# A streaming-encoder layer on one core: first two projection blocks split at token 256, loads re-ordered, square-root table loaded first

## What is computed

```python
def _rmsnorm(x, g):
    xf = x * rsqrt(mean(x * x, axis=-1) + EPS)
    return xf * g

h = _rmsnorm(x, norm_mix_pre)
c = h @ w_in        # 15 column blocks for RWKV-7, 12 for differential attention, 16 for the gates
```

## Time and profile before

| | us |
|---|---|
| median of 3 runs | 1066.26 (1065.84 to 1068.44) |
| the profiled execution, whole | 1068.19 |
| its span, first to last instruction | 1066.4 |
| PE busy / PEld busy | 1011.7 / 952.3 |
| DVE / ACT / POOL busy | 490.4 / 277.4 / 487.5 |
| granted TensorE clock, mean | 0.979 |

### The profile page before, as it was taken

The page is one execution under the profiler, slowest core; times in us unless marked ns, Lnnn a source line. Parts: engine busy times, 40 slices in busy tenths (PEclk is TensorE's granted clock), DMA queues, the critical chain, the costliest instruction groups (busy, mean ns, idle before and its releaser), DMA issues.

```text
span 1066.4 us, 21824 instructions
## 1 busy us (share of the span) xinstructions
PE 1011.7 (95%) x8886; PEld 952.3 (89%) x8886; DVE 490.4 (46%) x876; ACT 277.4 (26%) x782; POOL 487.5 (46%) x327
## 2 busy tenths in 40 slices
PE   4999999999879998989999999999999999999996
PEld 4999999977768887878799998999999999999996
DVE  5566799377767455555345254233323333200003
ACT  4223444345434123332211254010101010011101
POOL 3555566332215123142146811665655556566571
PEclk9999999999979999999889999999999999999998
DMA  7322323422213110103303621323323232322332
GB/s 240 84 81 79 84 76 81 132 81 71 64 33 85 43 32 13 52 32 115 109 26 119 190 73 41 96 81 88 89 80 97 79 98 79 91 79 86 92 90 85
DMA packets 137581, 89.16 MB, mean 84 GB/s; under 512 B 5242, under 2 KB 129504, under 8 KB 137504
## 3 DMA queue, kind: packets, MB, share of 16 engines
q1 hardware_dynamic: 128980, 72.65, 23.9%
q10 hardware_dynamic: 8524, 15.42, 4.2%
HBM read 78.86 MB, written 9.19 MB: 83 GB/s over the span
## 4 chain that ended last, share of the span: by engine, by line
PE 81%; DVE 12%; ACT 3%; issue 2%; POOL 1%; DMA 1%; ACTq 0%; DVEq 0%; POOLq 0%
PE dense L956 65%; PE side L1026 3%; PE side L882 1%; PE side L1146 1%; PE side L872 1%; DVE early L1645 1%; PE side L908 1%; PE side L1069 1%; PE side L938 1%; DVE amax L1629 1%; PE side L862 1%; DVE gt L1750 1%; DVE AR L1817 1%; ACT early L1260 1%; PE side L903 1%
## 5 line engine op out<-in xcount | busy, mean ns | idle before, releaser
L698 POOL TENSOR_SCALAR w_hi<-w_raw 128x1024 fp32r<-128x1024 f32 x117 | 128.0, 1094 | 440.5 <-PE dense L956 425.8
L956 PE MATMUL dense<-h_hi,w_hi 128*128 128x272 f32 (+1 forms) x1392 | 305.6, 297 | 7.9 <-DVE h_lo L1565 6.2
L956 PE MATMUL dense<-h_lo,w_hi 128*128 128x272 f32 (+1 forms) x1392 | 296.1, 290 | 0.0
L956 PE MATMUL dense<-h_hi,w_lo 128*128 128x272 f32 (+1 forms) x1392 | 294.7, 289 | 0.0
L701 POOL TENSOR_TENSOR w_lo<-w_raw,w_hi 128x1024 fp32r<-128x1024 f32 x117 | 285.7, 2442 | 9.8
L956 PEld LDWEIGHTS dense<-h_hi,w_hi 128*128 128x128 f32 x1392 | 222.2, 191 | 18.7 <-DVE h_lo L1565 6.9
L956 PEld LDWEIGHTS dense<-h_lo,w_hi 128*128 128x128 f32 x1392 | 224.1, 191 | 0.0
L956 PEld LDWEIGHTS dense<-h_hi,w_lo 128*128 128x128 f32 x1392 | 223.2, 191 | 0.0
L956 PE MATMUL dense<-S,w_hi 128*128 128x272 f32 (+2 forms) x648 | 109.3, 289 | 0.0
L956 PEld LDWEIGHTS dense<-S,w_hi 128*128 128x128 f32 x648 | 92.1, 188 | 0.1
L956 PE MATMUL dense<-S,w_lo 128*128 128x272 f32 (+2 forms) x324 | 68.2, 288 | 0.0
(11 more groups left out here) (265 smaller groups left out, 1423.6 us busy)
## 6 DMA issues: line engine op xcount, KB each, us to landing
w_raw<-in_w_ffn_in SPq DMA_DIRECT2D x44, 512.0 KB, 3.8
w_raw<-in_w_in SPq DMA_DIRECT2D x43, 512.0 KB, 3.9
w_raw<-in_w_ffn_out SPq DMA_DIRECT2D x16, 448.0 KB, 3.6
gates<-gst ACTq DMA_DIRECT2D x16, 272.0 KB, 2.0
w_raw<-in_w_o SPq DMA_DIRECT2D x8, 512.0 KB, 3.9
w_raw<-in_w_ffn_out SPq DMA_DIRECT2D x8, 512.0 KB, 3.8
mb<-gates ACTq DMA_DIRECT2D x1, 2176.0 KB, 10.7
ga<-gates ACTq DMA_DIRECT2D x1, 2176.0 KB, 10.8
```

The lines of the kernel that those rows point to most:

```text
L698: nc.gpsimd.tensor_scalar(hi, w_raw[:, slot, :], 1.0, 0.0, ALU.mult, ALU.add).then_inc(hi_split, 1)
L956: ins = pe.matmul(acc[:, bk, 0:tn], w, r[:, t0:t0 + tn], start=first and n == 0, stop=final and n == 2)
```

## The change

The two first blocks are cut at token 256 instead of 272. Their first part needs tiles 0 and 1 only, and it is 256 columns wide; the second is 288. In the list the first part of c0 moves to just behind B1, then come A3 and B2, the first part of c1, A4, B3, B4, and the two second parts. The list of ACT, DVE and POOL keeps its order; only PE's changes. SP issues x0, `gain`, x1, unit 0, x2, unit 1, x3, x4, and then the parameters. The squares throw their result into `tmp` in SBUF, so the wait for all square roots is gone. DVE sets `rms` to one at the start, ACT waits for it and takes a square root of it, ahead of the first square. ACT's three copies of the two blocks follow the new cut.

```diff
--- before.py
+++ after.py
@@ -198,16 +198,13 @@
 
         return [(st, i - k) for i in range(n + len(stages) - 1) for k, st in enumerate(stages) if 0 <= i - k < n]
 
-    def first_pair(steps, blocks):
-
-        halves = [("dense", *d, hf, BY_TOKENS) for hf in range(2) for d in blocks]
-        return steps[:-2] + halves[:1] + steps[-2:-1] + halves[1:2] + steps[-1:] + halves[2:]
-
     def spread(n, places):
 
         return [(i + 1) * n // places - i * n // places for i in range(places)]
 
-    s = first_pair(skew(NT, "normA", "normB"), [("c", i) for i in C_ORDER[:2]]) + [("params",)]
+    first_pair = [("dense", "c", i, hf, BY_TOKENS) for hf in range(2) for i in C_ORDER[:2]]
+    norms = skew(NT, "normA", "normB")
+    s = norms[:5] + first_pair[:1] + norms[5:7] + first_pair[1:2] + norms[7:] + first_pair[2:] + [("params",)]
     beside = {
         2: [("shift", CWA), ("loraW",)],
         3: [("shift", CK)],
@@ -526,7 +523,7 @@
     stored = sem("stored")
     kout_stored = [sem(f"kout_stored{i}") for i in range(2)]
     gate_stored = [sem(f"gate_stored{i}") for i in range(2)]
-    names = """ident_loaded x_sq x_normed x_hi cst_loaded small_loaded att_loaded gain_loaded lam_prod lam_exp
+    names = """rms_set ident_loaded x_sq x_normed x_hi cst_loaded small_loaded att_loaded gain_loaded lam_prod lam_exp
         smax sattn o_rms o_scaled o_hi_done shifted lora_a kinv shift_set rw_w rw_kk ksq ksqrt lora_g mb_loaded ga_loaded
         rw_g rw_p rw_gm rw_e2 rw_bo rw_done zeroed init_loaded g2_zeroed xb_init xp_init xe_set xb_last x64_diag x64_set
         y_sq y_rs y_aff y_gated y_hi_done mixed
@@ -651,12 +648,17 @@
             sp.dma_start(subln[:, :], i_["diff_subln"][0].partition_broadcast(P)).then_inc(s_["att_loaded"], 16)
 
 
-        for t in range(NT):
+        def x_load(t):
             sp.dma_start(xs[0:TILES[t][1], t, :], x_rows(t)).then_inc(x_sems[t], 16)
-            if t == 0:
-                sp.dma_start(gain[:, :], i_["norm_mix_pre"][0].partition_broadcast(P)).then_inc(s_["gain_loaded"], 16)
+
+        x_load(0)
+        sp.dma_start(gain[:, :], i_["norm_mix_pre"][0].partition_broadcast(P)).then_inc(s_["gain_loaded"], 16)
         for u, (kind, n, part) in enumerate(UNITS):
-            if u == 2:
+            if u < 2:
+                x_load(u + 1)
+            elif u == 2:
+                x_load(3)
+                x_load(SAMPLE)
                 load_parameters()
             slot = u % 2
             if FFN_UNIT0 <= u < DOWN_UNIT0:
@@ -963,9 +965,7 @@
             if parts_ == BY_TOKENS:
 
                 if kind == "c":
-                    landed(pe, ("normB", (2, SAMPLE)[part]), "n1")
-
-                    pe.wait_ge(s_["x_sq"], NT)
+                    landed(pe, ("normB", (1, SAMPLE)[part]), "n1")
                 else:
                     landed(pe, ("zC", (LATE, EARLY)[part][-1]), "n1")
             if kind == "outB":
@@ -1012,6 +1012,8 @@
                         places = [(0, *WO_PART[kind[-1]][0:2])]
                     elif kind in ("ug", "uv"):
                         places = [(1 - part, *WO_PART["AB"[part]][0:2])]
+                    elif parts_ == BY_TOKENS:
+                        places = [(part, *WO_PART["BA"[part]][0:2])]
                     else:
                         places = [(hf, hf * HALF, HALF) for hf in ((0, 1) if parts_ > 0 else (part,))]
                     ins = three(acc, hi, lo, rh, rl, p == 0 and n == 0, p == len(parts) - 1 and n == len(ops) - 1, places)
@@ -1206,6 +1208,8 @@
                 s_[name], 1)
 
         act.dma_start(ident[:, :], i_["cst"][:, K_ID:K_ID + P]).then_inc(s_["ident_loaded"], 16)
+        act.wait_ge(s_["rms_set"], 1)
+        A(f_act(rms[:, :], rms[:, :], ACT.Sqrt))
         for step in SCHEDULE:
             k = step[0]
             if k == "params":
@@ -1217,7 +1221,7 @@
                 t0, n = TILES[t]
 
                 act.wait_ge(x_sems[t], 16)
-                A(f_act(dps[0][0:n, :, :], xs[0:n, t, :].rearrange("p (a b) -> p a b", a=2), ACT.Square,
+                A(f_act(tmp[0:n, 0:2, 0:D // 2], xs[0:n, t, :].rearrange("p (a b) -> p a b", a=2), ACT.Square,
                         accum_out=ssq[0:n, t:t + 1]))
                 A.mark(f_act(rms[0:n, t:t + 1], ssq[0:n, t:t + 1], ACT.Sqrt, scale=1.0 / D, bias=EPS), s_["x_sq"], "x_sq")
             elif k == "normB":
@@ -1498,9 +1502,10 @@
                     f_act(qkv[:, i, :].rearrange("p (a b) -> p a b", a=2), acc[:, :, 0:HALF], ACT.Copy).then_inc(
                         block_sem(d), 1)
                 elif kind == "c":
-                    f_act(C[:, i, 1:1 + HALF], acc[:, 0, 0:HALF], ACT.Copy)
-                    f_act(C[:, i, 1 + HALF:1 + SEQ], acc[:, 1, 0:SEQ - HALF], ACT.Copy)
-                    f_act(C[:, i, 1 + JS:1 + J], acc[:, 1, SEQ - HALF:HALF], ACT.Copy).then_inc(block_sem(d), 1)
+                    cut = 2 * P if parts == BY_TOKENS else HALF
+                    f_act(C[:, i, 1:1 + cut], acc[:, 0, 0:cut], ACT.Copy)
+                    f_act(C[:, i, 1 + cut:1 + SEQ], acc[:, 1, 0:SEQ - cut], ACT.Copy)
+                    f_act(C[:, i, 1 + JS:1 + J], acc[:, 1, SEQ - cut:TOK - cut], ACT.Copy).then_inc(block_sem(d), 1)
                 elif kind in ("gA", "gB"):
                     col = PV_BG + i + (KT if kind == "gB" else 0)
                     n = i + (KT if kind == "gA" else 0)
@@ -1574,6 +1579,7 @@
                                      cst[0:n, K_BB:K_BB + nb].unsqueeze(2).unsqueeze(3).broadcast_to([n, nb, 64 // s, s]),
                                      ALU.mult), s_["xe_set"], "xe_set")
 
+        vec.memset(rms[:, :], 1.0).then_inc(s_["rms_set"], 1)
         for step in SCHEDULE:
             k = step[0]
             if k == "params":
```

## The result

| | before | after |
|---|---|---|
| median, measured side by side (8 runs each) | 1067.35 (1064.54 to 1068.74) | 1060.78 (1058.30 to 1063.46) |
| profiled execution, whole | 1068.19 | 1061.27 |
| its span | 1066.4 | 1059.4 |
| granted TensorE clock, mean | 0.979 | 0.984 |

All in us, but for the clock. The ratio is 0.9950, 95% interval 0.9932 to 0.9968: 5.3 us faster by the ratio, and 6.6 us by the medians. The kernel is faster, and by more than the forecast's 1.9 us.

The account below looks back on a forecast made before the run. PE was taken to bound the kernel from 38.16 us on. 3.52 + 0.12 + 0.18 - 1.72 = 2.10 us put unit 2 1.92 us earlier; less 0.03, 1.89 us off 1066.26 gave 1064.4 us, range 1062.2 to 1066.4 us.

Parts of the forecast that it names:

- the shift of unit 2: At POOL's split of unit 2 and PE's start on it: 1.92 us earlier, PE at 36.24 instead of 38.16 us.
- after that the same profile, shifted: Everything behind unit 2: unchanged, only moved earlier by the same time as unit 2.
- the 1.8 us around it are left as they are: Around the profiled span, 1066.4 us of 1068.19 us: these 1.8 us taken as unchanged.
- The first part's place in time: PE's start on c0's first part: 16.76 us, 3.52 us earlier, as it needs tile 1 and not tile 2.
- No collision: Rival at the start: POOL doesn't hold tile 2's `xn`, PE starts 1.5 us earlier, 1062.9 us; chance 0.10.
- The rival of mixed loads: Rival at the first loads: unit 0's packets pass beside x1's, x1 up to 1.6 us later, 1066.0 us; chance 0.13.
- the faster clock: Rival at c0's first part: PE's step short from its start, 2.1 us more saved, 1062.3 us; chance 0.15.
- the 4.92 us of the old trace: In c0's first part: time from first matmul until PE's step falls, carried over unchanged, a microsecond either way allowed.
- the narrower first part: c0's first part at 256 columns instead of 272: 5.25 us instead of 5.37 us, a gain of 0.12 us.
- The loss at the second parts: Gap ahead of c0's second part: 3.34 us instead of 1.62 us, B3 and B4 both falling in it; loss 1.72 us.
- The rival of the slow clock: Rival from c1's first part up to unit 2: steps at the long value, 6.8 us lost, 1071.2 us; chance 0.05.
- The table: Square-root table load on ACT, moved ahead of x0's arrival: taken as 0, bounds 0 and 0.3 us gained.

Follow-up runs that it names:

- e5: The changed kernel itself, run again beside before: 1060.9 us against 1065.18 us, ratio 0.9962.
- e1: The changed kernel with one GpSimd memset of 640 columns ahead of POOL's split of unit 2: -2.7 +/- 1.8 us against before, ratio 0.9972.
- e13: The changed kernel with 31 useless PE products, 23 between 280 and 300 us and 8 near 512 us: 1057.27 us, ratio 0.9925 against before.
- e16: The changed kernel with two writes of 810 columns on POOL ahead of its split of unit 2: -1.0 +/- 1.4 us against before, ratio 0.9993.
- e4: The changed kernel with the four parts of the first blocks back at their old places in PE's list: 1058.49 us, ratio 0.9938 against before.
- e2: The kernel before with three GpSimd memsets of 1000 columns ahead of the split of unit 2: +3.2 +/- 1.7 us against before, ratio 1.0028.
- e8: The kernel before with 23 useless PE products in its pauses between 289 and 304 us: 1061.08 us, ratio 0.9962 against before.
- e12: The kernel before with one useless memset of `rstd` more on DVE at its start: 1065.34 us, ratio 1.0013 against before.
- e14: The kernel before with the same 31 useless PE products as e13: 1058.06 us, ratio 0.9943 against before.
- e3: The changed kernel with the loads in their old order, all token tiles ahead of the weights: 1061.32 us, ratio 0.9971 against before.
- e9: The kernel before with the early square root alone: 1063.12 us, ratio 0.9991 against before.
- e10: The kernel before with the loads alone in their new order: 1066.41 us, ratio 1.0019 against before.
- e6: The changed kernel with useless transposes of the identity in PE's pauses at the start: 1059.58 us, -5.6 +/- 1.3 us against before.
- e7: e4 with useless transposes of the identity in PE's pauses at the start: 1058.58 us, -6.4 +/- 1.1 us against before.
- e15: e11 without the 8 useless products near 512 us: 1056.75 us, -8.9 +/- 1.3 us against before.
- e11: e7 with 31 useless PE products, 23 between 280 and 300 us and 8 near 512 us: 1050.95 us, ratio 0.9872 against before.

## Why the prediction was right and wrong

**The step that failed.** The forecast set the whole change of the time equal to the shift of unit 2, 1.89 us, and took that off a median of three runs. Its "after that the same profile, shifted" and "the 1.8 us around it are left as they are" put everything behind unit 2 at nothing, and the range had no term for the scatter of the level. The shift itself came out right, 1.8 us. What stands in place of those zeros is a level 1.1 us lower than the three runs gave, a mean granted clock that was higher in the changed kernel's runs, with which some 1.6 us go by an estimate below, and a last store that lands 1.0 us sooner in the traces.

**The first part's place in time: right.** 16.76 us was forecast; 16.57, 16.76, 16.73, 16.85 and 16.57 us stand in the five traces with the changed start (after, e5, e1, e13 and e16). Unit 0 landed at 9.78 us (9.3 to 9.8), its `w_lo` ended at 14.10 us (14.3). Of No collision nothing is left: the `xn` of tile 2 was held up in every one, 1.88 us in after and 2.74 us in e5. It makes little difference which engine gets in first, as said: in e5 the `xn` of tile 1 took 1.29 us and POOL's `w_hi` 2.11 us instead. The Trainium skill, page SBUF — State Buffer, section Who interferes with whom, says that DVE and GpSimd share a pair of ports as an exclusive lock, and that a DVE instruction with two inputs in SBUF contends with a GpSimd instruction that reads SBUF. The trace agrees: these `xn` take 1.88 to 3.00 us beside POOL's splits and 1.28 us alone. The rival of mixed loads fell too: x1 was squared at 8.07 us (7.99 before). So did the faster clock: c0's first part took 4.48 us or more in all five traces, where that rival would have made it some 3.1 us. The squares into SBUF took 1.06 us, as costed. A small slip of the sum: in the 4.92 us of the old trace PE began 21 matmuls, not 21.7, so that the narrower first part should gain nearly 0.2 us in place of 0.12 us.

**The loss at the second parts: right.** The time from the first of the moved transposes to c0's second part was forecast at 3.34 us; after shows 28.74 - 25.58 = 3.16 us. e4, whose second parts start 1.2 to 1.6 us earlier, confirms from the other side what it costs.

**Unit 2: right on the mean, wrong in the profiled run.** Single traces at either side scatter, so single traces should not be subtracted. In e1, e2 and e16 the figure is the start of the added writes, ahead of the delay:

| | POOL could have unit 2 at, us | mean |
|---|---|---|
| start of before (before, e2, e8, e12, e14) | 34.51, 34.26, 33.76, 33.73, 33.69 | 33.99 |
| changed start (after, e5, e1, e13, e16) | 33.85, 31.93, 31.52, 31.89, 31.84 | 32.21 |

1.8 us, where the sum had 1.92 us; by the spread within the two rows, the 1.8 us are good to about a microsecond. The scatter has two sources. The clock's rise within c0's first part moves its length from 4.48 us (e1) to 5.46 us (after), and from 4.92 us (e14) to 5.59 us (e2) with the old start; the forecast carried one trace's 4.92 us over and allowed a microsecond, which was right. And the clock fell ahead of the second parts in after and e3, two of six traces with this pause, for 1.5 us. The rival of the slow clock thus exists, at one time in three instead of 0.05, but at 1.5 us instead of 6.8 us: in after the step was back at 0.13 us by 32.2 us, before unit 2. The Trainium skill, page TensorE: Matmul & The Clock Gate, section What's actually happening, has idling bring the slow state back. The traces agree in part: here a pause of 1.5 us did so twice and failed to four times.

**"After that the same profile, shifted": not so in the profiled pair, and the traces can't decide it for the kernel.** From unit 2 to unit 116 before took 994.3 us, and e2, e9, e10 and e12, which run the same program from there on, 990.2, 987.2, 991.3 and 989.6 us: the mean of the five is 990.5 us. After took 988.9 us, and e1, e3, e4, e5, e6, e7 and e16 991.5, 990.4, 991.5, 992.6, 990.2, 990.0 and 994.7 us: the mean of the eight is 991.2 us. No gain of the changed kernel is seen there, but by the spread of either row the difference of the means is good to 3 us only. The profiled execution of before was itself 3.8 us above the mean of its kind, by its long low stretches, and none of the 5.3 us between the profiled pair can be put down to the change by traces.

**The clock over all runs: not in the sum.** Each run's mean granted clock is on record. In e5 it was 0.9851 in the mean, in the 31 runs of before beside it 0.9816: 0.0035 +/- 0.0015 higher. (The first comparison has after at 0.9849; the clocks of its runs of before are not on record.) What a clock is worth can be read from before alone: in its 126 runs of the later comparisons, those with a clock higher by 0.001 were 0.46 +/- 0.09 us faster. By this estimate 1.6 us of e5's 4.3 us are clock (2.1 us by what e8 and e14 gained for their higher clocks, 0.6 us for 0.001). The same working for the other comparisons, each with its delay added back:

| | gain by the means | of it clock, by this estimate | left |
|---|---|---|---|
| e5 | 4.3 | 1.6 | 2.7 |
| e1 and its delay | 3.4 | 0.9 | 2.5 |
| e16 and its delay | 2.7 | 0.4 | 2.3 |
| e13 against e14 | 1.9 | -0.7 | 2.6 |

What is left agrees among the four as the raw gains don't, and it is what the start (1.8 us) and up to 1.0 us for the last store can explain. Whether the higher clock is an effect of the change stays open: in e1 and e16, the same kernel delayed by 0.73 and 1.70 us, it is higher by 0.0020 +/- 0.0018 and 0.0008 +/- 0.0019 only.

**The level: wrong by 1 us.** The forecast took its gain off a median of three runs, 1066.26 us. Its eight runs beside after have 1067.35 us, and the 17 to 32 runs of each of the five later comparisons 1065.1, 1065.2, 1065.1, 1064.3 and 1065.4 us, while the changed kernel has 1060.8 and 1060.9 us. So what the first comparison shows more than the second lies in the runs of before. Three runs of a kernel with 2 us of scatter don't fix a level to better than 1 us, and no part of the range stood for it.

**The last store: not seen.** 1.0 us in the traces, with one more instruction on DVE; in e12's times it isn't there. The forecast took what lies around the span and its end as fixed. **The table**, costed at 0 with 0.3 us as bound, gave 1.9 +/- 1.3 us in e9, whose trace has 0.4 us of it at the first product against the like kernels, and 1.0 us at the last store. The first is just over the bound; the second is the accident above. By its ratio e9 can't be told from before.

**The whole, and what stays open.** The measured gains are, by the means, 6.6 +/- 1.7 (first comparison, of 8 runs), 4.3 +/- 1.2 (e5), 3.4 +/- 1.8 (e1 and its delay), 2.7 +/- 1.4 (e16 and its delay) and 1.9 +/- 1.8 us (e13 against e14). They don't all agree within their intervals: the first lies above the last two. Without it the other four, weighted by their intervals, give 3.3 +/- 0.7 us. From the 1066.26 us that the forecast started from to the 1060.78 us measured are 5.5 us. Of them 1.8 us were forecast and are borne out by the traces, 1.1 us were the level, some 1.6 us go with the higher clock, and up to 1.0 us with the last store. Each of these is good to a microsecond or so, so that their sum is no proof. Why the clock was higher, and whether the last store counts in the time, stays open. The start's mechanism and size held. The range didn't, because it was built from the start's uncertainties alone, when the level and the scatter of 2 us that the clock brings are larger. A width of 1 to 2 us more on each side, and a chance of faster near one in two, is what the same reading should have given. The information was there: PE idle for 4.2 us of 295 to 305 us in before, and a granted clock of 0.65 and 0.50 in the stretches behind, say that the time of this kernel hangs on things that no instruction of the change touches.

## What to carry to other kernels

Before subtracting one trace from another, ask of each stretch whether the program differs there; where it doesn't, a difference is scatter, and the same stretch of a second trace of the same kernel says how much. Put the scatter of the median into the range beside the terms of the sum: with gains of 0.2% it is the largest term. Compare the mean granted clocks of the two kernels' runs as well as their times: here a third of the gain went with the clock. And where PE stands still for a microsecond or more ahead of long PE-bound work, read the granted clock behind the pause: useless products put into the pause may be worth more than what a rearrangement saves.

## What the runs showed of the chip

- The granted clock falls to its lower level for some microseconds after pauses of PE, in places that differ from execution to execution. 31 useless products of 128 columns bought before 6.1 us (1058.06 us), and together with most of the change, the first parts at their old places and the start's pauses filled, 13.9 us (1050.95 us), more than twice what the change brings. A quicker start and a steadier clock add up, roughly: e7's 6.4 and e8's 4.3 us make 10.7 us, e15 has 8.9 us; e7's and e14's 6.1 us make 12.5 us, e11 has 13.9 us.
- Filled pauses don't always keep the clock up: at 525 to 535 us it was 1.00 in e14's trace and 0.63 in e13's, with the same products.
- Over 126 runs of one kernel, 0.001 more of the mean granted clock went with 0.46 +/- 0.09 us less.
- A pause of the same length may or may not bring the clock down: 1.5 us ahead of the second parts did in two of six traces.
- Warm from the start isn't warm for good: in e6 the transposes from 8 us on ran at the short length (1.10 us for eight instead of 1.94 us), PE was busy for 5.7 us of the 8 up to 16 us, and stood still for 2.28 us ahead of c0's first part. Its first matmuls stepped by 0.12 us (2.4 GHz), and from 17.9 us on by 0.213 us (1.2 GHz).
- A packet of the instruction queue in the last 4.2 us goes with a last store that SP waits for 1.0 us longer (3.3 against 2.3 us, in 5 traces against 13), and in e12's trace one instruction more on DVE moves it away. e12's times don't show the microsecond.
